# The order of VectorE's and ScalarE's work in the heads stage of a hybrid attention block

## The reference, cut to what matters

```python
h = rms_norm(x, norm_mix)
proj = h @ w_in                       # qa, ka, va, qb, kb, vb, forget logits
qa, ka = rms_norm(qa by 64), rms_norm(ka by 64)      # 8 heads, two maps each
p = softmax(q1 k1^T/8 + alibi) - lam * softmax(q2 k2^T/8 + alibi)   # chunk mask
oa = rms_norm(p @ va, subln_diff) * (1 - lambda_init)
qb, kb = rms_norm(qb by 128), rms_norm(kb by 128)    # 8 heads
ob = softmax(qb kb^T/sqrt(128) + F[t] - F[s]) @ vb   # causal, F = cumsum(log f)
gates = sigmoid(h @ w_gate + b_gate)
x = x + (g_diff * (oa @ w_branch_diff) + g_fox * (ob @ w_branch_fox)) @ w_out
x = x + relu(rms_norm(x, norm_mlp) @ w_mlp_up)**2 @ w_mlp_down
```

## Time and profile before

| | us |
|---|---|
| median of three runs (2799.61 to 2801.01) | 2800.96 |
| the profiled execution | 2801.55 |
| its span | 2799.8 |
| TensorE busy | 2726.6 (97%) |
| VectorE busy | 1754.5 (63%) |
| ScalarE busy | 1160.1 (41%) |
| heads stage with the tail | about 478 to 1088 |

### The profile page before, as it was taken

The page is one execution under the profiler, slowest core; times in us unless marked ns, Lnnn a source line. Parts: engine busy times, 40 slices in busy tenths (PEclk is TensorE's granted clock), DMA queues, the critical chain, the costliest instruction groups (busy, mean ns, idle before and its releaser), DMA issues.

```text
span 2799.8 us, 44340 instructions
## 1 busy us (share of the span) xinstructions
PE 2726.6 (97%) x15942; PEld 2410.6 (86%) x15942; DVE 1754.5 (63%) x3065; ACT 1160.1 (41%) x1563; POOL 36.0 (1%) x60
## 2 busy tenths in 40 slices
PE   8999999999999999999999999999999999999999
PEld 7999999777777778888889999999998888888887
DVE  4548887677777775443468787878774444454544
ACT  5534443444444344223344444444444343434333
POOL 0000000000000000000000000000000000000000
PEclk9999999999999999999999999999999999999999
DMA  7334444322222224444333434343447565666653
GB/s 249 108 119 128 135 127 120 90 68 68 67 63 67 68 68 129 142 143 143 121 128 128 135 127 135 122 135 126 135 130 253 194 226 187 198 216 201 218 197 118
DMA packets 359586, 387.20 MB, mean 138 GB/s; under 512 B 16448, under 2 KB 273984, under 8 KB 358976
## 3 DMA queue, kind: packets, MB, share of 16 engines
q1 hardware_dynamic: 331920, 347.24, 39.6%
q10 hardware_dynamic: 27568, 38.81, 3.9%
HBM read 348.23 MB, written 37.75 MB: 138 GB/s over the span
## 4 chain that ended last, share of the span: by engine, by line
PE 88%; DVE 6%; issue 3%; ACT 2%; DMA 1%; SPq 0%; DVEq 0%; ACTq 0%
PE job L1671 5%; PE job L1674 5%; PE job L1673 5%; PE scores L1974 2%; PE job L1974 2%; PE job L1978 2%; PE job L1976 2%; PE scores L1978 2%; PE scores L1976 2%; PE job L2001 2%; PE job L2003 2%; PE job L2002 2%; PE scores L2001 2%; PE scores L2002 2%; PE scores L2003 2%
## 5 line engine op out<-in xcount | busy, mean ns | idle before, releaser
L1608 DVE TENSOR_TENSOR w_lo_d<-raw_d,w_hi_d 128x512 fp32r<-128x512 f32 x256 | 176.2, 690 | 368.9 <-ACT w_hi_d L1031 368.9
L1347 DVE TENSOR_TENSOR lo<-pair,hi 128x1792 fp32r<-128x1792 f32 x142 | 287.1, 2022 | 125.2 <-ACT hi L809 125.2
L809 ACT ACTIVATE hi<-pair 128x1792 fp32r<-128x1792 f32 x142 | 241.5, 1700 | 272.3 <-PE heads_out L1978 118.7
L665 ACT ACTIVATE w_hi<-raw 128x512 fp32r<-128x512 f32 x272 | 171.0, 631 | 386.9 <-PE job L1674 268.5
L1031 ACT ACTIVATE w_hi_d<-raw_d 128x512 fp32r<-128x512 f32 x256 | 161.5, 632 | 405.5 <-PE heads_out L2003 202.8
L1086 DVE TENSOR_TENSOR w_lo<-raw,w_hi 128x512 fp32r<-128x512 f32 x272 | 188.9, 696 | 176.4 <-ACT w_hi L665 170.6
L1671 PE MATMUL job<-a_hi,w_hi 128*128 128x512 f32 x576 | 239.4, 416 | 2.9 <-DVE w_lo L1086 2.9
L1674 PE MATMUL job<-a_hi,w_lo 128*128 128x512 f32 x576 | 228.6, 397 | 0.0
L1673 PE MATMUL job<-a_lo,w_hi 128*128 128x512 f32 x576 | 227.9, 396 | 0.0
L1974 PE MATMUL scores<-h,hi 128*128 128x256 f32 x512 | 145.4, 284 | 4.7 <-DVE h L1540 2.6
L1614 DVE TENSOR_TENSOR u_lo<-u_raw,u_hi 128x2048 fp32r<-128x2048 f32 x64 | 146.2, 2284 | 4.5 <-ACT u_hi L1037 4.5
(11 more groups left out here) (449 smaller groups left out, 7782.4 us busy)
## 6 DMA issues: line engine op xcount, KB each, us to landing
pair<-in_w_mlp_up SPq DMA_DIRECT2D x256, 256.0 KB, 2.8
u_raw<-u_rows SPq DMA_DIRECT2D x64, 1024.0 KB, 5.6
raw_d<-in_w_mlp_down SPq DMA_DIRECT2D x128, 512.0 KB, 6.2
raw<-in_w_in SPq DMA_DIRECT2D x80, 512.0 KB, 4.1
pair<-in_w_gate SPq DMA_DIRECT2D x84, 256.0 KB, 2.9
raw<-in_w_out SPq DMA_DIRECT2D x64, 256.0 KB, 3.3
u_rows<-u_out ACTq DMA_DIRECT2D x32, 512.0 KB, 4.3
raw<-in_w_in SPq DMA_DIRECT2D x24, 344.0 KB, 3.2
```

Source lines behind the costliest of these rows:

```text
L665: nc.scalar.activation(w_hi[:, u % SPLITS], raw[:, slot, part:part + KU], ACT.Copy).then_inc(hi_ready, 1)
L809: nc.scalar.activation(pair_hi[j % 2], pairs[j][:, :, 1:8], ACT.Copy).then_inc(pair_hi_ready, 1)
L1347: nc.vector.tensor_tensor(pair_lo[j % 2], pairs[j][:, :, 1:8], pair_hi[j % 2].bitcast(F32), ALU.subtract).then_inc(pair_lo_ready, 1)
L1608: nc.vector.tensor_tensor(w_lo_d[:, j % SPLITS], raw_d[:, j // 2, j % 2], w_hi_d[:, j % SPLITS].bitcast(F32), ALU.subtract).then_inc(down_ ...
```

## The change

On VectorE `norm_step`, which makes a norm's factors, moves from the end of a step to right behind `scale_step`, ahead of the softmax work, the splits of q and k and the split of weights. On ScalarE `head_step` (bias copies, exponentials, the rounding of kind 1's output) moves ahead of `norm_step` (the takes for the norms and the rounding of q, k and kind 0's output). Both hold for the turns and for the tail. Since kind 1's output is now rounded first, VectorE's two waits on `o_hi` change their counts.

```diff
@@ ScalarE, heads_turn (the tail likewise)
-                    head_hooks(norm_step, u, i, work)
                     head_hooks(head_step, u, i, work)
+                    head_hooks(norm_step, u, i, work)
@@ VectorE, head_step
                 if kind == 1 and t == 23:
-                    dve.wait_ge(o_hi, i * 2 + 2)
+                    dve.wait_ge(o_hi, i * 2 + 1)
...
                 if kind == 0 and t == NORM_STEPS[0][2] + NORM_LENGTH + 1:
-                    dve.wait_ge(o_hi, i * 2 + 1)
+                    dve.wait_ge(o_hi, i * 2 + 2)
```

More of the change, by code:

```diff
@@ L874, in heads_turn @@
                         nc.scalar.activation(lf_t[:, 1], lf_t[:, 2], ACT.Ln).then_inc(f_ln, 1)
+                    head_hooks(head_step, u, i, work)
                     head_hooks(norm_step, u, i, work)
-                    head_hooks(head_step, u, i, work)
             heads_turn(0, HEADS)
@@ L894, in _ @@
                 round_unit(TAIL, u + LEAD)
+                head_hooks(head_step, u, H, TAIL)
                 head_hooks(norm_step, u, H, TAIL)
-                head_hooks(head_step, u, H, TAIL)
                 if u == 4:
@@ L1465, in _ @@
                 head_hooks(scale_step, u, H, TAIL)
+                head_hooks(norm_step, u, H, TAIL)
                 head_hooks(head_step, u, H, TAIL)
@@ L1468, in _ @@
                 split_unit(TAIL, u + LEAD)
-                head_hooks(norm_step, u, H, TAIL)
                 if u == 0:
```

## The result

The changed kernel takes 2813.6 us (median of five runs, 2811.84 to 2815.92) where the kernel before takes 2800.78 (five runs beside them): 1.0047 times, with a 95% interval of 1.0035 to 1.0058. It is 12.8 us slower. The profiled execution has a span of 2811.9 against 2799.8, so 12.1 us are to be found in it.

A forecast was written before the change was run, and what follows sets the result against it. TensorE, busy 97% of the span, was taken as the bound. 2801.55 us plus 0 for inner turns, 8.6 for the ends and 6.8 for clock falls made 2817, 2816 as a median; range 2799 to 2829, the forecast's own 2811 to 2822.

The forecast's parts named there:

- Step 12: TensorE waits 0.6 us for late squares, then about 2.2 us at step 13 for late probabilities.
- Step 14: The 3.82 us wait for the output norm's factors shrinks to 0.6; the next norm's squares come 3.7 us earlier.
- Steps 15, 0 and 1: Factors before the first block's probabilities make a new 3.4 us gap at step 0; of 3.7 us won, 1.2 remain.
- Steps 2 and 5: ScalarE's exponentials and bias copies delay the norms' squares; TensorE waits 1.2 us at step 2, 0.9 at step 5.
- The inner turn: A turn becomes 71.6 to 71.7 us against a mean of 71.70, so six inner turns come out at 0.
- The ends: Turn 0's forget sums +2.0, turn 0 to 1 +2.0, turn 7 to tail +2.2, tail's step 12 +2.4: +8.6 us.
- passage from turn 0 to 1: No wait at step 14 to win there, so steps 15 to 5 only lose: values about 2.0 us later.
- The clock: Of eight 2.2 us gaps at step 13, four lower TensorE's clock: +6.8 us; bounds 0 and 13.6.
- The first: Rival: the 2.2 us gaps at step 13 leave the clock alone, 2809.5 us; chance 0.20.
- the second: Rival: all eight gaps lower the clock, and step 0's low clock reaches past step 1, 2828 us; chance 0.17.
- The third: Rival: VectorE's loop turn costs nothing after a recent wait, 15.7 us back, 2794 us (2801 with four falls); chance 0.10.
- The fourth: Rival: the refilling of waits is smaller than worked out; 1 us a turn less means no change, 2803 us; chance 0.16.

The follow-up runs named there:

- e8: The changed kernel with VectorE's loop over the turns written out: 2812.98 us, 1.0044 times the kernel before.
- e1: VectorE's half of the change alone (factors first), ScalarE in the order of before: 2793.83 us, 0.9971 times the kernel before.
- e4: The changed kernel, but in turn 0 VectorE negates the forget sums at the start of step 5, ahead of the factors: 2811.15 us.
- e9: e7 with VectorE making the factors first at steps 5 and 9 and turn 0's forget sums early: 2744.11 us, 0.9793 times the kernel before.
- e3: The changed kernel, but at step 15 VectorE makes the factors at the step's end as before: 2807.88 us, 1.0023 times the kernel before.
- e7: e6 with VectorE's loop over the turns written out: 2746.98 us, 0.9808 times the kernel before.
- e5: The kernel before, with VectorE making the factors first at step 12 alone: 2776.65 us, 0.991 times the kernel before.
- e6: The kernel before with step 11's exponentials early on ScalarE; VectorE's step 12 makes probabilities, then factors, low part of k at step 13: 2770.78 us.

## Why the prediction was right, point by point

It said 2816 and slower; it is 2813.6, inside the forecast's own range of 2811 to 2822. The waits were worked out well; that the sum came so near is in part luck, since two terms were off by 3.7 and 1.6 us in opposite directions. By its steps:

**Step 12: right.** TensorE waits 0.53 for the squares (0.6 said) and 1.85 for the probabilities (2.2 said). The forecast's own figures give 1.9 for the second: TensorE was to reach the turning at 724.86 + 0.6 and to begin it at 727.4. The slip changed no other time, but it put the gap nearer to the middle between 1.5 and 2.7 us, and from there came the half of the eight that were taken to lower the clock.

**Step 14: right.** The wait of 3.8 is gone and the values run at full clock. Turning to next squares is 9.99 us (661.46 to 671.45); the forecast's 727.4 and 737.35 make 9.95.

**Steps 15, 0 and 1: right in the waits.** 3.29 at step 0 (3.4 said). At step 1 the forecast had VectorE late. The trace has no wait there, and e8 shows that TensorE's own low clock would have made it as late; VectorE's copy ends at 683.20 and TensorE turns at 683.35, so the two bounds all but coincide. The effect is the same, the reason only half the one that was given. That VectorE lets nothing pass, on which the sum rests, was read from one row without a wait; the rows of VectorE and ScalarE after, above, show it with a wait of 2.56 us.

**Steps 2 and 5: right.** 1.15 and 0.82 (1.2 and 0.9 said; for the second the forecast's own times, 766.35 less 754.5 and the 10.78 us between the squares in the earlier trace rows, make 1.1), both for L672. ScalarE's rows show the cause:

```profile
686.27 0.62 ACT L689 ACTIVATE side<-side,row_min 128x384 f32<-128x384 f32 x1 [2.83 <-DVE row_min L1161]
...
687.48 0.57 ACT L672 ACTIVATE main<-job 128x512 f32<-128x512 f32 x1
...
697.78 1.76 ACT L681 ACTIVATE main<-scores,neg_f 128x128 f32<-128x128 f32 x4
699.42 0.60 ACT L672 ACTIVATE main<-job 128x512 f32<-128x512 f32 x1
```

At step 2 ScalarE waits 2.83 us for logits, then makes two exponentials, with the copy of a product long finished behind them; at step 5 four bias copies do it. It is seen best against e1: take this half away and the time drops by 19.8 us.

**The inner turn: right.** 71.6 to 71.7 without a fall of the clock was said; it is 71.31, and 72.35 in a turn with a fall at step 13. The mean of six is 71.81 against 71.68 before, +0.8 in all. So the large change inside a turn nearly cancels, as was worked out (over the stage there are 13.5 us more of waits and 20 us less of low clock).

**The ends.** These rows of TensorE's timeline hold the passage from turn 0 to 1, and the starts of values in turn 1, in turn 7 and twice in the tail, beside the earlier trace rows:

```profile
529.05 0.60 PE L1682 MATMUL stats<-ident,main 128*128 128x128 f32 x4
...
534.50 0.33 PE L1727 MATMUL turned<-ident,side 128*128 128x128 f32 x1 [2.10 <-DVE side L1180]
...
563.08 2.32 PE L1765 MATMUL heads_out<-main 128*128 128x512 f32 x8
...
993.96 2.32 PE L1765 MATMUL heads_out<-main 128*128 128x512 f32 x8
...
1063.94 2.32 PE L1765 MATMUL heads_out<-main 128*128 128x512 f32 x8
...
1091.94 2.32 PE L1765 MATMUL heads_out<-main 128*128 128x512 f32 x8
```

| place | said | measured |
|---|---|---|
| before the stage's first squares | 0 | -1.4 |
| turn 0, and 0 to 1 (to the values of turn 1) | 2.0 + 2.0 | +5.9 |
| six inner turns, falls of the clock among them | 0 + falls | +0.8 |
| values of turn 7 to values of the tail | 2.2 + falls | +3.1 |
| to the last values of the tail | 2.4 | +2.6 |
| behind them | 0 | +1.0 |
| sum | 8.6 + 6.8 = 15.4 | 12.1 |

(The first row is the start of the first squares, 496.65, against 498.01 of the earlier trace rows; the others are differences of the same points in both traces. The first and the last row aren't the change's: ahead of the stage the trace before has a low stretch at 198.0 that the one after lacks, and behind it the trace after has two such stretches where the other has one. In all eleven traces the first squares stand at 497.9 to 498.1 with a low stretch ahead of the stage and at 496.4 to 496.7 without one. The stage alone is 12.4 us longer.) The forget sums cost 1.97 (2.0 said). **Mis-sized was the passage from turn 0 to 1**: 3.6 us instead of 2.0 (34.03 from 529.05 to 563.08, where it was 30.41). The gap at its step 0 was foreseen at 2.2 and is 2.10, but it lowered the clock, and the stretch after it was worked out at full clock. e4 shows that this was all: there the same gap left the clock alone, and the passage cost 2.1.

**The clock: the mis-sized term.** Eight gaps at step 13 were taken at 2.2 us with four falls of 1.7 us each; they are 1.85 long and three fell, at about 1.05 a turn (72.35 less 71.31). That is 3.1 us instead of 6.8, and these 3.7 are more than the whole difference between 15.4 and 12.1; the passage above gave 1.6 back. Four was a guess at the middle, and three came near it by luck: the same gaps lowered the clock one to three times of eight in six traces. The bounds, none and all, held.

**The rivals.** The first (no falls, 2809.5) is wrong by three falls; the second (all, 2828) by five. Its other half, a low stretch of step 0 that reaches past step 1, did not come in this trace, but it did twice in e1's (6.8 us long), and there the squares of step 2 came about 1 us later than in its other turns. The third put the loop's turn at nothing: VectorE still shows 1.97 to 2.19 us there, so it fell. But e8 adds what it missed: even without the loop's turn the changed kernel would gain nothing. The fourth, a smaller refilling, isn't seen: every wait is within 0.35 us of its size.

**Does the sum close?** The low clock takes 20 us less of the stage, yet TensorE's busy time is only 3.3 us less. Two things in the traces account for most of that. First, TensorE stood idle in part of the low stretches: it was busy in 52.3 us of the 58.0 before and in 36.5 of the 37.6 after. That is 15.8 less of work at half speed, worth 7.9. Second, a wait costs more than it is listed with. The last matmul ahead of the wait at 700.08 is this one:

```profile
698.87 0.39 PE L1674 MATMUL job<-a_hi,w_lo 128*128 128x512 f32 x1
```

It starts 0.23 us behind the one ahead of it (698.64), but is listed with 0.39. So to the start of the squares it is 1.21 us, 0.98 more than without the wait, where 0.82 are listed. Each of the 39 waits in the five rows after stands behind such a matmul, and there are 15 waits in the two rows before: 24 times 0.16 make 3.8 us. 7.9 less 3.8 leaves 4.1 against the 3.3 measured; the last 0.8 us are open.

## What to carry to other kernels

On an engine that works in order, what stands first in a step should be ready when the engine comes to it and wanted before the rest; sort each step by these two, not all steps by one rule. Here one of the five steps at which factors are made (12) carried 25 us of gain. The same move at all of them was worth 8, and with a swap on ScalarE that put exponentials ahead of a copy already due it became a loss of 13. (Of the other four, 5 and 9 did no harm in e9, and 15 cost 5.7 us in e3's comparison.) And before a stall on a helper engine is priced, look whether the main engine would be late there anyway: the same 2 to 2.7 us at each of six loop's turns were worth 24 us in one order and nothing in another.

## What was not expected of the hardware

- **The turn of a loop on VectorE.** 2.0 to 2.7 us idle with nothing waited for, once in each turn of a body of some 165 VectorE instructions (926 in 400 us); written out, it is gone (e7, e8). The Trainium skill, "Runtime: NRT & Kernel Launch", section "Instruction fetch mechanics", has a taken branch to code outside the prefetched window wait for a fetch of it. The runs agree with that; no other mechanism was tried against it, so that a fetch is the cause is not shown.
- **Gaps at the edge of the clock's fall.** Over the changed kernel, e1, e3, e4, e5 and e8 the same gap of 1.85 us at step 13 came 48 times and lowered the clock in 14 of them (3, 1, 2, 3, 2 and 3 of eight, in this order). In the nine traces with gaps of this kind (all but e7 and e9), those of 2.0 us (the forget sums) never did in four places, those of 2.10 did in three of four, and those of 2.7 to 4.1 in 69 of 72. The three that did not are 2.75 in e5 (at 603.42), 3.88 in e6 (602.58) and 3.30 in e8 (607.07). Those of 1.5 and less never did. So length alone does not decide, even for the long ones. What such a fall costs is seen in e5, where from squares to squares over step 1 it is 13.18 us without it and 14.86 with it, with gaps of nearly the same length (2.75 and 2.88). What parts the ones from the others is open.
- **A low clock lasts 3.4 or 6.8 us** in every stretch followed (before: nine of the one and four of the other; after: eleven of 3.4). With the gap at step 1 (e3) four of them were 6.8 long; with the gap at step 0 none were in the changed kernel, e4 and e8, but two were in e1. Why a stretch is long or short is open too.
